# Where the threshold search of a sparse attention stands: out of the index products, into the heads and the output projection

## The reference

```python
dots = jnp.einsum("bqhd,bld->bqhl", q_idx, k_idx) * (IDX_DIM ** -0.5)
s = jnp.einsum("bqh,bqhl->bql", w_idx * (N_IDX_HEADS ** -0.5), jax.nn.relu(dots))
scores = jnp.where(valid, s, -jnp.inf)          # 8 indexer heads of 64
_, sel = lax.top_k(scores, n_sel)               # 256 keys of each query
# attention of 8 query heads over the selected keys alone
p = jax.nn.softmax(jnp.where(valid, q @ k_sel.T * HEAD_DIM ** -0.5, -jnp.inf))
```

## Time and profile before

| | |
|---|---|
| median of 3 executions | 2611.46 us (2609.06 to 2613.33) |
| the profiled execution, its own time | 2617.17 us |
| its span, first to last instruction | 2615.4 us |
| mean granted clock of TensorE, share of full speed | 0.85 |
| TensorE busy | 2233.5 us, 85% of the span |
| VectorE busy | 1492.2 us, 57% |
| ScalarE busy | 1161.4 us, 44% |
| phase B | from about 697 to about 2351 us of the span |

### The profile page before, as it was taken

How to read it: one execution, slowest core, us unless ns; L and a number is a source line. 1 busy time by engine, 2 the same in 40 slices (tenths; PEclk the granted TensorE clock), 3 DMA queues, 4 the chain that set the end, 5 groups by cost and what they waited for, 6 DMA issues and landing times.

```text
span 2615.4 us, 34415 instructions
## 1 busy us (share of the span) xinstructions
PE 2233.5 (85%) x12592; PEld 1762.7 (67%) x12592; DVE 1492.2 (57%) x3449; ACT 1161.4 (44%) x2297; POOL 135.5 (5%) x174
## 2 busy tenths in 40 slices
PE   7999999999478888888988878888878888988765
PEld 4777777776466666676676666666666767768652
DVE  2444444443145666776787777878777842434580
ACT  1111111011025566665776766767577668432000
POOL 0000000000000000000000000000000010100004
PEclk9999999999567788777898989888889889987556
DMA  7111111111511110111011010101010010114001
GB/s 264 66 72 50 70 65 71 47 66 40 180 49 59 53 57 20 50 57 45 17 57 32 28 50 11 49 11 49 11 33 27 17 43 9 43 65 138 1 3 31
DMA packets 58411, 137.57 MB, mean 53 GB/s; under 512 B 13904, under 2 KB 26872, under 8 KB 57248
## 3 DMA queue, kind: packets, MB, share of 16 engines
q1 hardware_dynamic: 56096, 125.26, 14.3%
q0 software_dynamic: 2176, 10.49, 1.2%
HBM read 96.83 MB, written 38.90 MB: 52 GB/s over the span
## 4 chain that ended last, share of the span: by engine, by line
PE 62%; DVE 15%; ACT 13%; issue 6%; DMA 2%; SPq 1%; POOL 1%; PEld 1%; DVEq 0%; ACTq 0%; POOLq 0%; PEldq 0%
PE psum L566 12%; PE psum L599 9%; PE psum L1220 8%; PE psum L1189 7%; PE psum L1231 6%; PE psum L1212 5%; ACT sb_lowj L851 4%; PE psum L1178 3%; PE psum L1202 3%; DVE sb_junk L968 3%; ACT sb_ptb L838 2%; DVE sb_sc L953 2%; ACT sb_p L909 1%; PE psum L613 1%; DVE sb_p L987 1%
## 5 line engine op out<-in xcount | busy, mean ns | idle before, releaser
L1220 PE MATMUL psum<-sb_v,sb_ptb 128*128 128x64 f32 x2176 | 329.9, 300 | 31.0 <-ACT sb_ptb L838 30.6
L1220 PEld LDWEIGHTS psum<-sb_v,sb_ptb 128*128 128x128 f32 x2176 | 315.2, 221 | 49.4 <-ACT sb_ptb L838 48.9
L566 PE MATMUL psum<-sb_w,sb_xt 128*128 128x512 f32 (+5 forms) x1088 | 324.8, 459 | 0.5 <-DVE sb_xt L382 0.5
L851 ACT ACTIVATE sb_lowj<-sb_sc,sb_ncand,sb_scl 128x384 bf16<-128x384 f32 (+13 forms) x224 | 312.5, 1395 | 2.4
L968 DVE TENSOR_SCALAR_CACHE_REDUCE sb_junk<-sb_sc,sb_c 128x384 bf16<-128x384 f32 (+13 forms) x210 | 310.1, 1477 | 3.6
L1212 PE MATMUL psum<-sb_con,sb_p 128*128 128x128 f32 x1280 | 243.6, 320 | 52.6 <-ACT sb_p L909 31.3
L838 ACT ACTIVATE sb_ptb<-psum 128x512 f32<-128x512 f32 (+3 forms) x352 | 187.2, 533 | 185.0 <-PE psum L1212 183.8
L566 PEld LDWEIGHTS psum<-sb_w,sb_xt 128*128 128x128 f32 (+1 forms) x1088 | 178.5, 185 | 134.5 <-issue 125.1
L1231 PE MATMUL psum<-sb_wo,sb_mix 128*128 128x512 f32 x512 | 257.2, 666 | 13.5 <-DVEq L1146 13.5
L1189 PEld LDWEIGHTS psum<-sb_qa,sb_w 128*128 128x128 f32 x2048 | 250.7, 196 | 12.8 <-issue 4.8
L1189 PE MATMUL psum<-sb_qa,sb_w 128*128 128x128 f32 x2048 | 253.0, 280 | 1.3
(11 more groups left out here) (340 smaller groups left out, 2491.4 us busy)
## 6 DMA issues: line engine op xcount, KB each, us to landing
qt_s<-sb_qt SPq DMA_DIRECT2D x32, 512.0 KB, 2.8
sb_x<-in_x_prompt SPq DMA_DIRECT2D x16, 512.0 KB, 3.7
xt_s<-sb_xt SPq DMA_DIRECT2D x16, 512.0 KB, 2.6
sb_qa<-xt_s SPq DMA_DIRECT2D x16, 512.0 KB, 3.3
sb_qa<-qt_s SPq DMA_DIRECT2D x16, 512.0 KB, 3.5
sb_qa<-qt_s SPq DMA_DIRECT2D x32, 256.0 KB, 4.7
sb_xres<-in_x_prompt SPq DMA_DIRECT2D x16, 512.0 KB, 5.1
out_y_prompt<-sb_y SPq DMA_DIRECT2D x16, 512.0 KB, 3.0
```

What stands on the lines that cost most here:

```text
L566: mm = pe.matmul(out, m.xt[:, p, k, 0:n], m.w1[:, k, lo:hi], start=(k == 0), stop=(k == KD - 1))
L851: ins = act.activation(m.lowj[:, 0:w], m.sc[u % 3][:, 0:w], ACT.Sign, bias=m.ncand[:, p], scale=m.scl[:, p], accum_out=m.tally[:])
L1220: mm = pe.matmul(o, m.ptb[:, g, x * P:(x + 1) * P], v, start=st, stop=sp)
```

## The change

Three edits, no other code. VectorE makes no search while the index products are accumulated; all 15 are given out over the eight heads. ScalarE makes no low-bit operation between the Relus, where it made three per chunk of 512 columns; behind the third copy of a head it makes one more, so that heads with three or more chunks (attention rows of more than 1024 columns, from step 10 on) have four operations instead of three. What is left lies in the tail. The order within the 15 and within the 47 stays, and so does every result.

```diff
--- before.py
+++ after.py
@@ -870,8 +870,6 @@
                         if 2 * count + e > 3:
                             act.wait_ge(s.acc, 2 * count + e - 3)
                         act.activation(m.r[:, e, 0:c[1]], m.score(slot)[:, e, 0:c[1]], ACT.Relu).then_inc(s.relu, 1)
-                    if hp < 3:
-                        q = refine(u, q)
         else:
             for _ in range(12):
                 q = refine(u, q)
@@ -911,7 +909,7 @@
             q = refine(u, q)
             for n, c in enumerate(chunks(w, 512)):
                 take_group(("t", j, h, c))
-                if n < 2:
+                if n < 3:
                     q = refine(u, q)
         while indexed(u) and q < LOW_OPS:
             q = refine(u, q)
@@ -1078,10 +1076,7 @@
         done = 0
         if indexed(i + 1):
             for c in chunks(width(i + 1), 512):
-                if indexed(i):
-                    search(i, done, c, 0)
-                    done += 1
-                for h in range(3 if indexed(i) else 0, NIH):
+                for h in range(NIH):
                     accumulate(i + 1, c, h)
             dve.wait_ge(s.acc, 2 * scores.of[("D", i + 1, c, NIH // 2 - 1)][3])
         elif indexed(i):
```

## The result

| | before | after |
|---|---|---|
| median | 2610.26 us (2609.05 to 2613.33, 4 executions) | 2662.77 us (2659.49 to 2668.22, 4 executions) |
| ratio, 95% interval | | 1.0204, 1.0184 to 1.0225 |
| profiled execution, its span | 2617.17, 2615.4 us | 2668.22, 2666.3 us |
| TensorE's mean granted clock | 0.85 | 0.854 |

The change costs 52.5 us by the medians and 51.1 by the two profiled executions, where I forecast 44 (my terms added up to 43). I begin again with the page of the changed kernel: part 4's shares, then the transposes (L1207, L1212 before) and the index products (L1173, L1178 before), whose last column is TensorE's idle time ahead of them.

A forecast was written before the change was run, and what follows sets the result against it. It took VectorE's order of searches ahead of each head's maximum to bound the heads. Heads +32, sections +6 and ScalarE +5 made 43; on the 2611.5 us median it predicted 2656 us, range 2627 to 2690.

The forecast's parts named there:

- What bounds the heads: Heads: the next maximum waits behind VectorE's further searches, so order sets the time, not busy share; +32 us over all heads.
- 4 x P2: Heads 3 to 7: four times VectorE's maximum-to-maximum time with two searches, 26.4 us in step 12; +27 us in sum.
- Each waiting for the maximum: Heads 3 to 7, step 12: exponentials some 26.4 us apart instead of 22.4, each starting only after VectorE's maximum.
- ScalarE's second Sign: Heads 0, 3 and 6: two Signs, hidden by VectorE to step 14, then +3 per step at most, +5 for steps 15 and 16.
- Heads 0 to 3: Heads 1 and 2: one more search ahead of head 3's maximum, partly hidden by a wait; 4.5 us, about 1 each in steps 10 to 13.
- The sections: Index products and gates: steps 11 to 14 gain 8 us, others lose through longer tails; +6 in sum, +3 of it step 15.
- 2.9 - 1.95 = +1: Fourth pair of index products, step 12: four more ScalarE tail operations cost 2.9, the count ahead saves 1.95; net +1 us.
- the shift: Step 10's section: three more triples in the tail, 6.6 us, less the count of 1.7, pass to the fourth pair: +4.9.
- The rival of the clock: Heads of steps 8 to 13: waits take TensorE to 1.2 GHz, 36 us more, 2690 us; chance 0.20.
- Half of it: Heads' maxima slip by less and sections 6 to 10 hide their tails: 18 us, 2630 us; chance 0.09.
- faster: Heads' VectorE idle time swallows the searches, sections of steps 11 to 14 close by 8 us each: 2592 us; chance 0.04.
- it cancels: Sections of steps 11 to 14 gain 6 us each instead of 2, with half the head term: about 2615 us; chance 0.04.

The follow-up runs named there:

- late_gap: Kernel before, with the section's 1 to 4 searches per step moved behind the last head, up to three ahead of the attention output: 2611.49 us, 0.9998.
- v_only: Kernel before, with only VectorE's searches moved out of the section, all 15 in the heads, ScalarE unchanged: 2631.65 us, 1.008.
- third_copy: Kernel before, with only the fourth low-bit operation per head behind its third copy, from step 10 on: 2621.62 us, 1.0044.
- V: Edit of the kernel before: no VectorE search in the section, all 15 in the heads; alone 2631.65 us, 1.008.
- v_and_section: Changed kernel without its fourth low-bit operation per head: no search and no low-bit operation in the section: 2679.33 us, 1.0263.
- S: Edit of the kernel before: no ScalarE low-bit operation between the Relus; alone 2677.07 us, 1.0249.
- T: Edit of the kernel before: a fourth low-bit operation in a head, behind its third copy; alone 2621.62 us, 1.0044.
- step15: Kernel before, with step 15's four searches alone moved behind the last head, three ahead of the attention output, one ahead of hand-over: 2599.56 us, 0.9959.
- late_after: Kernel before, with all searches of the section moved behind the last gated block, ahead of hand-over and select: 2623.51 us, 1.0056.
- late_fit: Kernel before, with three or four section searches per step moved, in steps 10 to 14 only, into VectorE's idle stretches behind the last head: 2602.57 us, 0.9963.
- late_fit15: Kernel before, with the searches of steps 10 to 14 and step 15's four moved into idle stretches behind the last head: 2581.84 us, 0.99.
- s_section: Kernel before, with only ScalarE's low-bit operations taken out of the section into the tail: 2677.07 us, 1.0249.

## Why the prediction was right or wrong

The time came out near the forecast in part by luck: heads 3 to 7 lost 4 us more than I had, heads 0 to 3 7.4 more and the last stretch 11.2 more, and the sections gained 13.6 more, of which 4.0 in step 2 are none of the change's.

**What bounds the heads** held: the order on VectorE and not the busy share. Heads 3 to 7 came within 0.8 us of 4 x P2 in each step shown, 31.7 us against 28, and late_gap shows that the same searches behind the last head cost the heads nothing. The Trainium skill, "PSUM — Partial Sum Buffer", in "Engine vs sequencer instructions", says that the queues of ScalarE, VectorE and GpSimd are strictly first in, first out; the trace agrees (the mask that leads to the next maximum begins at 1731.65, as the count of 1729.78 with its 1.95 us ends, with no idle time between). By the idle share of VectorE alone they would have been free; v_only measured +24 us. "Each waiting for the maximum" holds in v_only and, in the changed kernel, up to step 9, where the maxima of heads 4 to 6 end 0.03 or 0.04 us before the exponentials. From step 10 on it holds in one to three of the five heads 3 to 7; in step 12 the exponential of head 4 begins 1.1 us after its maximum, because the second Sign of head 3 delays it. There the four heads take 7.26, 6.05, 6.06 and 7.26 us, not 6.59 each, and third_copy, without a moved search, has 7.26, 6.06, 5.75 and 7.26. So in steps 10 to 14 the sum of 4 x P2 is met, but V's place is shown by v_only and late_gap, not by the changed kernel's time.

**ScalarE's second Sign** was sized rightly for steps 15 and 16 (5.4 against 5), and it was right that VectorE hides it up to step 14. What I did not see is that it would take VectorE's place at the same price, 4 us in step 12.

**Heads 0 to 3** were undersized: 11.9 against 4.5. Of this 4.4 is step 6, where no term of mine stands; v_and_section has the same 4.4 there, and V alone and S alone have none of it. The window of its first three heads in the changed kernel:

```profile
1058.80:1074.50 15.70, 14.55 (x73) 12.79 (x73) 9.57 (x30) 9.26 (x26) 0.00 (x0) 0.65 0.07 18
```

The same in the kernel before:

```profile
1054.00:1065.20 11.20, 9.70 (x72) 8.48 (x72) 7.84 (x26) 9.09 (x25) 0.00 (x0) 1.00 0.10 27
```

TensorE has 73 and 72 pieces of work in them, at 0.65 and at 1.00; the whole difference is busy time of TensorE, 14.55 us against 9.70, at the lower clock. Why it falls there with V and S together is open. The 4.5 us that I gave to VectorE's search in steps 10 to 13 came out as 8.4, and mostly not by VectorE: v_only has 0.9 there and third_copy 9.9. In step 11 head 0 takes 10.33 us in the changed kernel and 10.32 in third_copy, where v_only has 8.71 and before 8.11: it is the second Sign of head 0, for which I had no term up to step 14.

**The sections** failed in the sum: with the stretch behind them +6 was forecast, and -4.1 measured without step 2. The select was to come 3 to 7 us later against the end of the projection; in steps 10 to 14 it came 4.9, 0.6, 0.5, 3.1 and 3.2 us later. "2.9 - 1.95 = +1" for the fourth pair is right where nothing else moves: it begins 1.0 and 1.1 us later after the section's start in steps 13 and 14. In steps 11 and 12 it comes earlier, by 1.1 and 1.4. The select there, on VectorE of the changed kernel:

```profile
1643.67 0.15 DVE L1054 TENSOR_SCALAR sb_fix<-sb_way 128x1 f32<-128x1 f32 x1 [6.91 <-ACT sb_way L854]
```

The fourth pair on TensorE:

```profile
1662.79 1.25 PE L1173 MATMUL psum<-sb_ks,sb_qi 128*128 128x512 f32 x4 [3.25 <-ACT sb_r L872]
```

The tail took 12.4 us instead of the 9.3 of before, where I had costed 2.9 more. But the projection beside it took 16.4 us instead of 14.0 (its clock 0.85 instead of 1.00), so the select stands only 0.5 us later against the section's start (7.7 us ahead of it; before 8.2), and 0.5 - 1.95 = -1.4. Also the pair now runs at the higher clock, 1.25 us against 2.08. The same in step 10: from head 7 to the end of the projection step 9 takes 1.7 us longer, so the shift is 4.9 us and not 6.6, less the count 3.3, and TensorE's wait goes from 0.78 to 4.10 us. Behind the fourth pair the sections of steps 11 to 14 gained 3.2 to 3.8 us each where I had 2.5.

**The last 11 us**, from head 7 to the end of the projection, I had left out: nothing of the change stands there in front of TensorE. What the rows show is a lower clock. Windows of the changed kernel in step 12, head 6 and then the stretch from the exponential of head 7 to the projection:

```profile
1740.50:1747.70 7.20, 5.39 (x40) 4.56 (x39) 7.09 (x14) 6.61 (x11) 0.00 (x0) 1.00 0.23 74
1747.70:1760.60 12.90, 9.34 (x43) 8.79 (x43) 3.33 (x7) 10.50 (x21) 0.00 (x0) 0.56 0.00 1
```

0.56 where before has 0.65 in 12.2 us. The runs do not give these us to one edit. V alone has 8.9 and S alone 0.4; but T alone, which moves no search, has 10.9 in steps 2 to 16 and 5.8 less in step 17. Step 11 is T's: +4.1 in the changed kernel and in third_copy, 0.0 in v_only. In it the transposes of head 7 wait 2.52 us for their exponential instead of 0.97, though they begin at the same 1.5 us behind its start, and the projection then runs at 0.85. Some 3.5 us more in step 14 belong to no edit at all: every run but step15 has 2.7 to 5.0 there, late_after and late_fit too.

**The rival of the clock** did not come: heads 3 to 6 stay at 1.00 in steps 10 to 14, in step 12 with TensorE busy 5.39 of 7.20 us, and the mean clock is 0.854. In steps 8 and 9 it fell from 0.95 to 0.88 and 0.91, and the heads kept 4 x P2 even so. The clock did cost in other places, and gave back in the sections. **Half of it** fell by the same rows; **faster** by v_only, and by all other combinations of the three edits, none of which is faster than before; **it cancels** by the sections of steps 11 to 14, which gained 3.7 us each and not 6, and by the full price of the heads.

What stays open: what lets the clock fall behind the last head and in step 6, and how much of the 12 us by which late_fit missed its expectation is the clock's: against late_gap its sections of steps 11 and 12 are short of 9.3 us (one count still stands in step 11) and those of steps 13 and 14 better by 2.8, 3.5 us stand behind head 7 of step 14 and 2.8 in the first heads of step 12.

## What to carry to other kernels

A small piece of work between two steps of a pipeline is priced by what stands behind it in its engine's order, not by the engine's busy share: the same searches cost 30 us ahead of the maxima and nothing behind the last one. Before moving work into idle time, list that idle time place by place, with what it waits for, and fill each no further than its length: with three searches in a 4.5 us gap, step 11 of late_gap gave back 5.7 of the 7.6 us that its shorter section had won. And test the edits of a change in all combinations: here V cost 24, S 70 and T 13 us, and all three together 52. A difference of one per cent between two kernels can hold as much luck as effect: in its profiled execution, late_fit15 has 12 us from places where its code is that of late_fit.

## What the runs showed of the hardware

The same matmuls of the projection of step 11 took 14.0 us at a granted clock of 1.00 (before), 15.7 at 0.89 (s_section) and 16.7 at 0.84 (late_gap); the wait ahead of them was 1.06 us in the first two, so the clock was not a matter of that wait alone. In the heads of the changed kernel the granted clock stayed at 1.00 from head 3 to head 6 of step 12 although TensorE had idle time in each of them; head 4, with TensorE busy 4.50 of 6.00 us:

```profile
1728.40:1734.40 6.00, 4.50 (x38) 4.30 (x38) 5.89 (x14) 5.25 (x11) 0.00 (x0) 1.00 0.00 1
```

The profiled executions of before and of step15, which differ in step 15 alone, agree to 0.1 us in every stretch of steps 3 to 14; the large differences outside step 15 sit in two places, 3.6 us in step 2 and 5.9 us between the last head and the projection of step 17. The profiled execution of late_fit15 has the code of before up to step 9, and yet differs from it by 4.0 us in heads 0 to 3 of step 8 and by 3.1 in heads 3 to 7 of step 7.
